# Splitting the residual update of a decoder step between VectorE and GpSimd

## The reference

```
def _rmsnorm(x, g):
    xf = x.astype(jnp.float32)
    xf = xf * lax.rsqrt(jnp.mean(xf * xf, axis=-1, keepdims=True) + NORM_EPS)
    return (xf * g.astype(jnp.float32)).astype(x.dtype)

def _layer(x, pos, st, lp):
    h = _rmsnorm(x, lp['norm_mix_pre'])
    y, new_st = _token_mixers(h, pos, st, lp)
    x = x + _rmsnorm(y, lp['norm_mix_post'])
    h = _rmsnorm(x, lp['norm_mlp_pre'])
    u = jnp.square(jax.nn.relu(jnp.einsum('btd,df->btf', h, lp['w_up'])))
    x = x + _rmsnorm(jnp.einsum('btf,fd->btd', u, lp['w_down']), lp['norm_mlp_post'])
    return x, new_st
```

## Time and profile before

| | us |
|---|---|
| Median of 3 runs | 3183.47 |
| Lowest and highest | 3183.3 and 3186.64 |
| The profiled execution | 3181.26 |
| Its span, first to last instruction | 3179.7 |
| PE busy in the span | 3103.3 |
| VectorE busy | 1903.6 |
| ScalarE busy | 1529.9 |
| GpSimd busy | 85.6 |

### The profile page before, as it was taken

One profiled execution on the slowest core, in us unless ns is written; L12 is line 12 of the kernel. 1 busy time (PEld: TensorE's weight loads), 2 busy tenths in 40 slices (PEclk: granted clock), 3 DMA queues, 4 the chain that ended last, 5 costly groups with the idle time before them and its releaser, 6 DMA issues.

```text
span 3179.7 us, 68177 instructions
## 1 busy us (share of the span) xinstructions
PE 3103.3 (98%) x23264; PEld 3050.6 (96%) x23264; DVE 1903.6 (60%) x3926; ACT 1529.9 (48%) x3564; POOL 85.6 (3%) x163
## 2 busy tenths in 40 slices
PE   8999999999999999999999999999999999999997
PEld 7999999998999999999989999999989999999997
DVE  6667776656545545455576777766565455454555
ACT  5467776544434333333454777755444333343333
POOL 1100000000000000000001000000000000000000
PEclk9999999999999999999999999999999999999998
DMA  5544444553444444545435444455534444444444
GB/s 195 163 141 141 144 141 155 178 166 127 166 168 160 167 164 160 170 159 166 152 124 180 145 137 140 134 166 161 167 125 166 166 164 161 164 165 167 163 161 149
DMA packets 266378, 499.69 MB, mean 157 GB/s; under 512 B 34304, under 2 KB 39584, under 8 KB 266208
## 3 DMA queue, kind: packets, MB, share of 16 engines
q1 hardware_dynamic: 243360, 443.56, 42.5%
q0 software_dynamic: 14784, 51.05, 4.7%
q10 hardware_dynamic: 8064, 2.80, 0.3%
HBM read 475.30 MB, written 22.01 MB: 156 GB/s over the span
## 4 chain that ended last, share of the span: by engine, by line
PE 89%; DVE 5%; ACT 3%; issue 1%; DMA 1%; DVEq 0%; POOL 0%; ACTq 0%; SPq 0%; POOLq 0%
PE PU L508 78%; PE PABCD L508 5%; PE PF L508 3%; PE PE_ L508 2%; ACT Y L857 1%; DVE WL L1230 1%; DMA RAW<-in_w 1%; PE PABCD L511 1%; ACT AE L857 1%; ACT WH L857 1%; PE PE_ L511 1%; DVE AE L1588 1%; DVE Y L1244 1%; DVE X L1247 0%; DMA Z<-in_gw 0%
## 5 line engine op out<-in xcount | busy, mean ns | idle before, releaser
L508 PE MATMUL PU<-HH,WH 128*128 128x288 f32 x4096 | 1277.4, 312 | 8.4 <-DVE WL L1230 8.4
L857 ACT ACTIVATE WH<-RAW 128x512 fp32r<-128x512 f32 x1669 | 961.8, 620 | 579.6 <-PE PU L508 428.5
L508 PE MATMUL PU<-HL,WH 128*128 128x288 f32 x4096 | 1209.6, 295 | 0.0
L508 PE MATMUL PU<-HH,WL 128*128 128x288 f32 x4096 | 1205.7, 294 | 0.0
L1230 DVE TENSOR_TENSOR WL<-RAW,WH 128x512 fp32r<-128x512 f32 x1668 | 1075.3, 686 | 196.8 <-ACT WH L857 183.9
L508 PEld LDWEIGHTS PU<-HH,WH 128*128 128x128 f32 x4096 | 771.9, 188 | 22.6 <-issue 7.5
L508 PEld LDWEIGHTS PU<-HL,WH 128*128 128x128 f32 x4096 | 773.2, 189 | 6.0
L508 PEld LDWEIGHTS PU<-HH,WL 128*128 128x128 f32 x4096 | 772.3, 189 | 0.0
L508 PE MATMUL PU<-UH,WH 128*128 128x288 f32 x2560 | 759.0, 296 | 2.8 <-DVE UL L1390 2.0
L508 PE MATMUL PU<-UL,WH 128*128 128x288 f32 x2560 | 755.2, 295 | 0.0
L508 PE MATMUL PU<-UH,WL 128*128 128x288 f32 x2560 | 752.7, 294 | 0.0
(11 more groups left out here) (246 smaller groups left out, 2224.4 us busy)
## 6 DMA issues: line engine op xcount, KB each, us to landing
RAW<-in_w SPq DMA_DIRECT2D x1669, 256.0 KB, 3.8
SIN<-in_sin POOLq DMA_DIRECT2D x32, 512.0 KB, 4.3
out_sout<-Y POOLq DMA_DIRECT2D x32, 512.0 KB, 5.5
BC<-gate_rows POOLq DMA_DIRECT2D x32, 304.0 KB, 4.1
AUX<-in_aux POOLq DMA_DIRECT2D x32, 152.0 KB, 3.1
X<-in_x SPq DMA_DIRECT2D x4, 576.0 KB, 8.5
out_y<-X SPq DMA_DIRECT2D x4, 576.0 KB, 2.8
out_sout<-SOUT ACTq DMA_DIRECT2D x32, 64.0 KB, 2.3
```

The costliest lines, as they stand in the source:

```text
L508: return nc.tensor.matmul(out, lhsT, rhs, start=start, stop=stop, skip_group_check=True)
L857: return nc.scalar.activation(out, in_, f, **kw)
```

## The change

VectorE keeps the first five pairs of chunks of each update (`LATE` is 5). The last three pairs, six chunks, go to GpSimd. GpSimd takes two instructions for each pair, both over 576 elements in each partition: `Y` times `RS`, then `X` plus `Y`. The norm weight, which VectorE's scaling instruction applied in the same pass, is multiplied into `Y` for these six chunks by ScalarE, right behind the square of the chunk. A second semaphore, `x_updated_late`, counts GpSimd's pairs, and all who wait for a pair go by `x_ready`. The three looped quads of "out" and of "down_last" are written out for PE, ScalarE and VectorE, so that the chunk is known in the code. Two pairs of semaphores are merged (`gdn_dx2` into `gdn_dx`, `ret_rows_out` into `rows_out`). At the end of layer 0 GpSimd issues the gate weight loads after its first update.

```
-                with eng.Fori(1, NC_ // 4) as j:
+                for j in range(1, NC_ // 4):
                     quad(q0 + HEADS + j, "out", l, (0, j))
...
-                with eng.Fori(1, NC_ // 4) as j:
+                for j in range(1, NC_ // 4):
                     quad(base + 12 + 8 * q + j, "down_last", l, (q + 1, j))
...
+        def x_ready(update, g):
+
+            if g < LATE:
+                return sem("x_updated"), LATE * update + g + 1
+            late = NC_ // 2 - LATE
+            return sem("x_updated_late"), late * update + g - LATE + 1
...
-                sp.wait_ge(sem("x_updated"), 16 * DEPTH + 2 * g + 2)
+                sp.wait_ge(*x_ready(2 * DEPTH, 2 * g + 1))
+                if 2 * g + 1 == LATE:
+                    sp.wait_ge(*x_ready(2 * DEPTH, 2 * g))
...
+            def update_late(e):
+
+                held("rs_ready", e + 1)
+                held("output_squares", SQUARES * (e + 1))
+                for g in range(LATE, NC_ // 2):
+                    k = slice(2 * g, 2 * g + 2)
+                    n = (NC_ // 2 - LATE) * e + g - LATE + 1
+                    pool.tensor_tensor(Y[:, k], Y[:, k], RS[:].unsqueeze(1).to_broadcast([128, 2, T]), ALU.mult)\
+                        .then_inc(sem("y_scaled_late"), 1)
+                    pool.wait_ge(sem("y_scaled_late"), n)
+                    pool.tensor_tensor(X[:, k], X[:, k], Y[:, k], ALU.add).then_inc(sem("x_updated_late"), 1)
...
+                update_late(2 * l)
                 if l < DEPTH - 1:
                     load_gate_weights(l + 1)
+                update_late(2 * l + 1)
...
-                fn(dst, Y[:, bass.ds(c, 1)].rearrange("p a t -> p (a t)"), ACT.Square).then_inc(sem("output_squares"), 1)
+                fn(dst, Y[:, c], ACT.Square).then_inc(sem("output_squares"), 1)
+                if c >= 2 * LATE:
+
+                    gain = NG[:, 0 if kind == "out" else 2, c:c + 1]
+                    if c == 2 * LATE:
+                        act.wait_ge(sem("gains_in"), 16 * (l + 1))
+                    fn(Y[:, c], Y[:, c], scale=gain).then_inc(sem("output_squares"), 1)
...
                 for g in range(8):
-                    update_x(l, which, gain, g)
+                    if g < LATE:
+                        update_x(l, which, gain, g)
                     if g:
                         prenorm_lo(lo_l, lo_which, lo_gain, range(2 * g - 2, 2 * g))
```

More of the change, by code:

```diff
@@ L45 @@
 MLP_Q = D_FF // D_MODEL
+LATE = 5
+LATE_CHUNKS = NC_ - 2 * LATE
+SQUARES = NC_ + LATE_CHUNKS
 SLOTS = 32
@@ L317, in halves, with squares_before @@
             return a[:, 0:HD].rearrange("p (a g c) -> p a g c", a=2, c=FIRST_BLOCK * 2 ** lev)
+        def x_ready(update, g):
[3 more added lines that the diff above has]
+            return sem("x_updated_late"), late * update + g - LATE + 1
+        def squares_before(c):
+            return c + max(0, c - 2 * LATE)
         def ul_before(l, kind, q):
@@ L467, in _ @@
             pool.sem_inc(sem("states_stored"), 1)
+            pool.sem_inc(sem("x_updated_late"), NC_ // 2 - LATE)
             for name in ("prompt_out", "norm_out", "cnew_out"):
@@ L471, in _ @@
             for l in range(DEPTH):
-                pool.dma_start(d["bc"][l * HEADS + H_C:l * HEADS + H_C + H_B], d["k_rows"]).then_inc(sem("ret_rows_out"), 16)
-            held("ret_rows_out", 16 * DEPTH)
+                pool.dma_start(d["bc"][l * HEADS + H_C:l * HEADS + H_C + H_B], d["k_rows"]).then_inc(sem("rows_out"), 16)
+            held("rows_out", 16 * DEPTH)
             for l in range(DEPTH):
@@ L557, in output_sum @@
             def output_sum(e):
-                pe.wait_ge(sem("output_squares"), NC_ * (e + 1))
+                pe.wait_ge(sem("output_squares"), SQUARES * e + squares_before(NC_ - 1) + 1)
                 pe.wait_ge(sem("squares_added"), (NC_ - 2) * (e + 1) + 1)
@@ L885, in prenorm @@
                         act.wait_ge(sem(f"x_in{g // 2}"), 16)
-                    act.wait_ge(sem("x_updated"), 16 * l + 4 * e + g + 1)
+                    act.wait_ge(*x_ready(2 * l + which, g))
                     for c in (2 * g, 2 * g + 1):
@@ L905, in output_squares @@
                 e = 2 * l + (0 if kind == "out" else 1)
-                if not isinstance(x[1], int):
+                if x[1]:
                     act.wait_ge(sem("squares_added"), (NC_ - 2) * e + c - 3)
@@ L1105, in gdn_head @@
                         fn(DX[:, a:b], bc[:, a:b], ACT.Relu, bias=CUR[:, j, 3:4]).then_inc(sem("gdn_dx"), 1)
-                    act.wait_ge(sem("gdn_dx"), 3 * (nk + 1))
+                    act.wait_ge(sem("gdn_dx"), 6 * nk + 3)
                     fn(DX, DX, ACT.Exp, scale=-1.0).then_inc(sem("gdn_decay"), 1)
                     for j, (a, b, m) in enumerate(TILES):
-                        fn(SC[:, a:b], bc[:, a:b], ACT.Relu, scale=-1.0, bias=CUR[:, j, 0:1]).then_inc(sem("gdn_dx2"), 1)
-                    act.wait_ge(sem("gdn_dx2"), 3 * (nk + 1))
+                        fn(SC[:, a:b], bc[:, a:b], ACT.Relu, scale=-1.0, bias=CUR[:, j, 0:1]).then_inc(sem("gdn_dx"), 1)
+                    act.wait_ge(sem("gdn_dx"), 6 * nk + 6)
                     fn(SC[:, 0:T], SC[:, 0:T], ACT.Exp, scale=-1.0).then_inc(sem("gdn_decay2"), 1)
@@ L1657, in add_square @@
                 e = 2 * l + (0 if kind == "out" else 1)
-                dve.wait_ge(sem("output_squares"), NC_ * e + c + 1)
+                dve.wait_ge(sem("output_squares"), SQUARES * e + squares_before(c) + 1)
                 if not isinstance(c, int) or c > 1:
@@ L1685, in mixer @@
                     gates(t, -1 if kind == "first" else x[2], l)
-                if kind == "down_last" and isinstance(x[1], int) and l < DEPTH - 1 and t in (9, 17):
+                if kind == "down_last" and x[1] == 0 and l < DEPTH - 1 and t in (9, 17):
                     gate_weights(l + 1, t // 16)
@@ L1745, in after_mlp @@
                 else:
-                    for g in range(8):
+                    for g in range(LATE):
                         update_x(l, 1, NG[:, 2], g)
-                dve.wait_ge(sem("x_updated"), 8 + 16 * l + 16)
+                dve.wait_ge(sem("x_updated"), LATE * (2 * l + 3))
                 dve.sem_inc(sem("layer_free"), 1)
@@ L1758, in _ @@
             dve.sem_inc(sem("squares_added"), 1)
-            dve.sem_inc(sem("x_updated"), 8)
+            dve.sem_inc(sem("x_updated"), LATE)
             walk(dve, split_first, quad, after_out, after_mlp)
```

8 lines of the change are left out of this document (4 added, 4 removed).

## The result

| | before | changed |
|---|---|---|
| median, us (lowest to highest, runs) | 3183.39 (3181.33 to 3186.64, 4) | 3206.79 (3205.71 to 3207.28, 4) |
| ratio to before, 95% interval | | 1.0072 (1.0059 to 1.0085) |
| span of the profiled execution, us | 3179.7 | 3205.7 |

The changed kernel is slower by 23 us, 0.7%. 3179.3 was forecast, with 3194 as the upper end of the range.

What follows compares the result with a forecast made beforehand. PE bounds the kernel, except at the program's end, where VectorE's updates count whole. Terms -3.3 (end), -0.5 (WL wait) and -0.4 (written-out loops) sum to -4.2 us: 3179.3 on the median, range 3176.5 to 3194.

Steps and rivals of the forecast that it cites:

- The first five pairs stay as they are: At the three places with PE behind them, VectorE's first five pairs and PE's 4.23 us wait were to stay unchanged.
- Rival A: At all four places VectorE and GpSimd take turns reading SBUF: +9.6 us, 3193, with P = 1.0; chance 0.25.
- P: Time of one GpSimd instruction over 576 elements, at all four places; taken between 0.76 and 1.5 us.
- 2P to 5P: Rival A's cost at each of three places, from GpSimd instructions ahead of the first X and first HL; PE pays all.
- 8.3 + 6P against 13.3: Rival A's end of the program: both engines' times add; +1.0 us with P = 1.0.
- B (VectorE first): At the update places VectorE goes first and GpSimd gets only the gaps: +1.8 us, 3185; chance 0.15.
- C: At the update places GpSimd is slow by itself: 3185 with P = 2.5, 3199 with P = 3.9; chance 0.12.
- The end of the program, -3.3: After VectorE's fifth pair the last store lands at 3176.0 against 3179.3, if GpSimd is done by 3173.0.
- The 0.50 us wait for WL: At the first place PE's wait for the last WL goes; nothing at the second and third: -0.5 us.
- The loops written out: Register work on counts goes from the chain to RS at four places: 0 to -0.7 us, taken as -0.4.
- ScalarE's multiplications: ScalarE's 24 more instructions, 0.45 us each, fall in its idle time at the four places: cost nothing.
- the moved gate weights' loads: The 1 MB loads move from 653 to about 755, where the DMA share is 0.12: cost nothing.

Runs made afterwards that it cites:

- the runs with fills: Changed kernel with GpSimd's six instructions replaced by memsets that only write, so the last six chunks aren't updated: ratio 0.9982 to the kernel before.
- PSUM operands: Changed kernel with RS also written to PSUM for VectorE's scaling, and scaled Y to PSUM at the last place: ratio 1.0033 to the kernel before.
- the one-input run: Changed kernel with GpSimd's instructions each multiplying one tensor by a constant, so the last six chunks aren't updated: ratio 1.0014 to the kernel before.
- the last-place run: Changed kernel with VectorE alone at the first three places; GpSimd's three pairs beside VectorE's PSUM operands only at the last: ratio 0.9998 to the kernel before.
- the run with the six instructions on VectorE: Changed kernel with GpSimd's six instructions done by VectorE after its own five pairs, ScalarE's multiplications kept: ratio 0.9995 to the kernel before.
- the run that held it back: Changed kernel with GpSimd waiting for VectorE's third pair at the first three places, its fifth at the last: ratio 1.0074 to the kernel before.

## Why the prediction was wrong

**The first five pairs stay as they are: wrong, and this is the step that failed.** The sum took VectorE's and GpSimd's instructions as independent and started GpSimd just when PE waits for the first pair. Each GpSimd instruction holds up one of VectorE's by 1.1 us, 6.7 us at a place. PE waits for 5.2 of them: 2.2 us ahead of the first squares and 3.0 ahead of the first HL, which had some time to spare. Its second stop costs 2.5 more in the restart, most of it for the lower clock, and 0.8 comes back from the WL stop. The runs on operands show the cause: take away GpSimd's reads, or VectorE's second SBUF operand, and the holds are gone; leave both and only move them in time, and the cost stays.

The Trainium skill (SBUF — State Buffer, Who interferes with whom) has this rule, reads against two SBUF inputs and not writes, and the runs with fills and with PSUM operands agree with it; the one-input run does in part only, its additions weren't held up. By the Trainium skill (SBUF — State Buffer, Summary: rules for kernel authors) the one that comes second blocks until the other has finished. A hold measured here is 1.1 us, beside a GpSimd instruction of 1.40 us alone and 1.44 to 1.92 in company; no row shows at what point of it VectorE goes on.

**Rival A** named the mechanism and had 0.25. It was priced at 3P with P = 1.0, 3193, and all six instructions fell ahead of the first HL that PE needs. With the upper end of its 2P to 5P and the measured P of 1.40 the sum is 3 x 7.0 + 3.4 - 0.4 = +24.0, 3207.5. That this meets the measured 3206.79 is luck, put together after the result. The 7.0 at a place are 5.2 us of waiting and 2.5 of restart, less 0.8, and A's working has no term for the restart. The end of the program, 8.3 + 6P against 13.3, was +3.4 by it and measured +3.23, for other reasons again: VectorE ends only 15.1 us after its start, 1.8 later than before, since a hold is 1.1 us and not P, and the other 1.5 us are the last two stores, which go out together and so land later, a term that stands in the forecast and not in A.

```profile
3200.26 0.76 DVE L1284 TENSOR_TENSOR X<-X,Y 128x576 f32<-128x576 f32 x1
```

```profile
L409 SPq DMA_DIRECT2D out_y<-X x4: 332/346/432, 3195.0 to 3201.5; - x4
DMA to landing us min/median/max: 2.8/2.8/3.9
```
B (VectorE first) is refuted, since VectorE is held up from its first pair on; C too: P is 1.40 us alone, inside the 0.76 to 1.5 that was taken.

**The end of the program, -3.3.** The stores' part was right: 3.47 us less where GpSimd is early. (Rows 9 have 16 slices with data and not 17, 1.5 us and not 1.6, and delaying each other by twice that leaves 1.7 and not 1.9; neither changes the reading.) But the term held "as long as GpSimd is done by 3173.0, P up to 1.5", and the end of GpSimd's own program was not counted. With 6.5 us from there, GpSimd would have to be done by 3179.7 - 3.3 - 6.5 = 3169.9, P under 1.0. At 1.40 the gain of three pairs is 0.8 even undisturbed, as the last-place run shows.

**The small terms.** The 0.50 us wait for WL is gone in the changed kernel, which proves little, since PE comes there 7 us later. It is gone too where VectorE's five pairs are undisturbed, in the run with the fills, and the place takes 28.88 us against 29.56: 0.7 for the 0.5 that was forecast. The loops written out gave 0.7 us in all for 0.4. ScalarE's multiplications and the moved gate weights' loads cost nothing that shows, as forecast. The place-by-place gain could not be told in the time of the run with the six instructions on VectorE (0.9995), so its -0.5 and -0.4 rest on the traces.

**The chances.** 0.42 for the forecast leaned on a trace in which GpSimd computes nothing. Such silence bears out neither case; the 0.40 for A and B was too little where the code shows two-operand reads on both engines at the moment that PE waits.

## What to carry to other kernels

Before work is split between VectorE and GpSimd, count the operands that each instruction reads from SBUF. If both read two, what runs together takes turns, so give VectorE a PSUM operand, or start GpSimd where VectorE has gaps (only at the last place of the run that held it back was it seen to work so, alone); moving it within a full stretch moves the loss only. A second stop of PE costs more than its length, since PE works at half clock again after it (2.5 us here beside 5.2 of waiting in all). At the end of a program, count 6.5 us from GpSimd's end as well as the landing of the last store.

## What the runs showed of the hardware

- GpSimd's two-operand instruction over 128x576 floats takes 1.39 to 1.40 us alone, 1.84 times VectorE's addition, and 1.44 to 1.92 us beside VectorE's SBUF reads; a fill of the same size takes 0.58.
- The two engines alternate finely: no VectorE instruction is late by more than about 1.2 us, and 6.7 us for VectorE go with 1.3 us for GpSimd (9.7 us for six instructions against 8.4).
- A GpSimd instruction with one SBUF input (128x576) took 1.65 to 2.09 us beside VectorE, where the one with two inputs took 1.44 to 1.92; it held up one of each two of VectorE's 288-element instructions by 0.4 us and its 576-element addition not at all.
- VectorE's scaling with an operand in PSUM takes 502 ns, to PSUM 515, against 512 in SBUF: the way round costs nothing but ScalarE's second write of RS, 0.45 us for whoever waits for the SBUF copy.
- The span ends 6.5 us after GpSimd's last instruction if nothing else is later, in five traces of this case (6.48 to 6.57 us); in a sixth, where GpSimd ends with a bare wait for VectorE, 6.8 us after VectorE's last addition.
- After a stop PE works at a granted clock of 0.50 for a while: for some 3.3 us after the first wait of 4.23 us in the kernel before, and for some 6 us after the second wait in the changed kernel, though PE is busy all that time.
